# Router stage of a two-layer transformer step: the order of tile turns, adaLN parts, slot counts and gate spreads

## The reference, cut to what matters

```python
mod = silu(c) @ w_mod[l] + b_mod[l]          # 6 vectors of 1024: shift1, scale1, gate1, shift2, scale2, gate2
...
x = x + gate1 * (merged @ lp['w_out'])
h2 = rms_norm(x, lp['norm2_w']) * (1 + scale2) + shift2
y = grouped_moe(h2, router_w, router_b, w_g, w_u, w_d)
x = x + gate2 * y
...
def grouped_moe(h, router_w, router_b, w_g, w_u, w_d):
    s = sigmoid(h @ router_w)                # 16 experts in 4 groups
    sb = (s + router_b).reshape(T, 4, 4)
    # the group with the largest sum of its best two; in it the best two experts
    # w = s of these two, divided by their sum
    for e in range(16):
        y = y + gates[:, e:e+1] * ((silu(h @ w_g[e]) * (h @ w_u[e])) @ w_d[e])
```

## Time and profile before

| | us |
|---|---|
| median of 3 runs | 1649.46 (1648.64 to 1653.35) |
| span of the profiled execution | 1646.0 |
| PE busy | 1567.6 (95%) |
| DVE busy | 1047.2 (64%) |
| ACT busy | 923.8 (56%) |
| POOL busy | 530.5 (32%) |
| layer 0: end of dense matmuls, first expert matmul | 486.3, 524.7 |
| layer 1: the same | 1300.2, 1335.0 |

### The profile page before, as it was taken

The page is one execution under the profiler, slowest core; times in us unless marked ns, Lnnn a source line. Parts: engine busy times, 40 slices in busy tenths (PEclk is TensorE's granted clock), DMA queues, the critical chain, the costliest instruction groups (busy, mean ns, idle before and its releaser), DMA issues.

```text
span 1646.0 us, 21287 instructions
## 1 busy us (share of the span) xinstructions
PE 1567.6 (95%) x7693; PEld 1234.8 (75%) x7693; DVE 1047.2 (64%) x1385; ACT 923.8 (56%) x1284; POOL 530.5 (32%) x271
## 2 busy tenths in 40 slices
PE   7999999989999999999889999999999989999996
PEld 4677778877775887888676777787767778888885
DVE  2226546673355898998862357377433479899998
ACT  3343445434335788888644343444353458888893
POOL 2344554444532111111234445444445131111112
PEclk9999999999998999999999999999999999999998
DMA  9765343344359999999946543422443469999995
GB/s 363 265 199 167 115 128 91 102 130 143 115 174 334 344 385 362 370 377 364 368 170 210 187 154 112 133 90 89 144 147 111 157 224 379 378 368 378 381 368 205
DMA packets 153822, 381.77 MB, mean 232 GB/s; under 512 B 21060, under 2 KB 26886, under 8 KB 153724
## 3 DMA queue, kind: packets, MB, share of 16 engines
q1 hardware_dynamic: 122704, 325.32, 56.2%
q10 hardware_dynamic: 20140, 36.56, 6.3%
q0 software_dynamic: 10880, 18.59, 3.1%
HBM read 378.55 MB, written 27.93 MB: 247 GB/s over the span
## 4 chain that ended last, share of the span: by engine, by line
PE 70%; DVE 12%; DMA 10%; ACT 5%; issue 2%; ACTq 0%; SPq 0%; POOL 0%; DVEq 0%; POOLq 0%
PE ps L606 56%; PE ps L615 4%; DVE wxl L2466 4%; DMA raw<-w_e_down 4%; DMA raw<-w_e_up 3%; PE ps L639 2%; PE ps L952 2%; ACT wxh L1826 1%; DMA own<-w_mod 1%; PE ps L980 1%; PE ps L886 1%; DVE uv L2241 1%; ACT wh L1331 1%; PE ps L658 1%; PE ps L650 1%
## 5 line engine op out<-in xcount | busy, mean ns | idle before, releaser
L1949 POOL TENSOR_TENSOR wl<-raw,wh 128x1024 fp32r<-128x1024 f32 x168 | 409.8, 2443 | 531.7 <-ACT wh L1331 531.5
L2466 DVE TENSOR_TENSOR wxl<-raw,wxh 128x1024 fp32r<-128x1024 f32 x384 | 454.5, 1220 | 55.2 <-ACT wxh L1826 52.5
L1826 ACT ACTIVATE wxh<-raw 128x1024 fp32r<-128x1024 f32 x384 | 402.6, 1061 | 92.4 <-DMA raw<-w_e_down 35.4
L606 PE MATMUL ps<-wxh,xeT 128*128 128x512 f32 x1024 | 341.3, 399 | 4.0 <-issue 2.5
L1331 ACT ACTIVATE wh<-raw 128x1024 fp32r<-128x1024 f32 x168 | 176.7, 1056 | 227.6 <-PE ps L606 223.2
L606 PE MATMUL ps<-wh,hTh 128*128 128x512 f32 x720 | 293.2, 407 | 5.9 <-DVE hTl L2088 3.3
L606 PE MATMUL ps<-wh,hTl 128*128 128x512 f32 x720 | 281.9, 392 | 0.0
L606 PE MATMUL ps<-wl,hTh 128*128 128x512 f32 x720 | 281.5, 391 | 0.0
L606 PEld LDWEIGHTS ps<-wxh,xeT 128*128 128x128 f32 x1024 | 193.3, 189 | 46.8 <-issue 4.3
L606 PE MATMUL ps<-wxl,xeT 128*128 128x512 f32 x512 | 199.9, 390 | 0.0
L606 PEld LDWEIGHTS ps<-wh,hTh 128*128 128x128 f32 x720 | 135.7, 188 | 40.7 <-issue 7.9
(11 more groups left out here) (282 smaller groups left out, 2177.3 us busy)
## 6 DMA issues: line engine op xcount, KB each, us to landing
raw<-w_e_gate SPq DMA_DIRECT2D x128, 512.0 KB, 6.5
raw<-w_e_up SPq DMA_DIRECT2D x128, 512.0 KB, 5.8
raw<-w_e_down SPq DMA_DIRECT2D x128, 512.0 KB, 5.5
raw<-w_in SPq DMA_DIRECT2D x120, 512.0 KB, 3.7
own<-w_mod ACTq DMA_DIRECT2D x27, 1024.0 KB, 7.6
raw<-w_mod SPq DMA_DIRECT2D x36, 512.0 KB, 5.1
raw<-w_br_b SPq DMA_DIRECT2D x16, 512.0 KB, 3.8
raw<-w_out SPq DMA_DIRECT2D x16, 512.0 KB, 3.8
```

The costliest lines, as they stand in the source:

```text
L606: ins = pe.matmul(out, act_hl[i], w_hl[j], start=start and n == 0, stop=stop and n == 2)
L1826: act.activation(wxh[:, q % RING_MOE, :, :], raw[:, place, :, :], ACT.Copy).then_inc(sem("hi_done"), 1)
L1949: pool.tensor_tensor(wl[:, p % RING, :, :], raw[:, PAIR_CHUNK[p] % RAW, :, :], wh[:, p % RING, :, :].bitcast(F32), ALU.subtract).then_inc( ...
L2466: dve.tensor_tensor(wxl[:, q % RING_MOE, :, :], raw[:, expert_chunk(l, 0, q)[0], :, :], wxh[:, q % RING_MOE, :, :].bitcast(F32), ALU.subtr ...
```

## The change

The diff touches the router stage alone, in both layers, and no size. Tile t's turn now comes as soon as PE reaches it behind the dense matmuls, and the adaLN parts stand between the tiles. ACT takes all eight columns of tile 0 (`ACT_COLUMNS`), with a semaphore `tile_whole` for the last four, and works on tile 0 ahead of the third tile's squares; DVE keeps columns 4 to 7 of tiles 1 and 2. The sigmoid's table and the `iota` load now follow the last `tile_front`. In layer 0 parts of blocks 2 and 3 come behind the token logits; in layer 1 three of the four gate spreads come behind the token sums. `counts` comes right behind the third tile's `back` (layer 1, with four spins ahead) or behind part(3, 0) (layer 0).

```diff
-FILL_ROUTER = (4, 4, 4, 6, 16)
+FILL_ROUTER = (4, 16)
+ACT_COLUMNS = (8, 4, 4)
...
             # PE, ahead of everything else of the stage
-            if more:
-                part(0, 0)
-                part(0, 1)
-                part(1, 0)
-                part(1, 1)
-            else:
-                part(10, 0)
-                part(10, 1)
-                part(11, 0)
...
             # PE, the stage's order (more: layer 0)
+            turn_tile(0)
             if more:
-                turn_tile(0)
+                part(0, 0)
+                part(0, 1)
                 turn_tile(1)
+                part(1, 0)
                 turn_tile(2)
-                part(2, 0)
+                part(1, 1)
                 logits(0)
+                logits(1)
                 turn_small(l + 1)
+                logits(2)
                 block_columns(blocks, 0)
-                logits(1)
-                part(2, 1)
-                logits(2)
-                block_columns(blocks, 1)
-                part(3, 0)
                 token_logits()
                 back(0)
                 back(1)
+                block_columns(blocks, 1)
+                part(2, 0)
+                part(2, 1)
+                back(2)
+                part(3, 0)
+                counts()
                 part(3, 1)
-                back(2)
                 block_columns(blocks, 2)
-                counts()
                 part(10, 0)
                 block_columns(blocks, 3)
             else:
-                spin(FILL_ROUTER[0], 2)
-                turn_tile(0)
-                spin(FILL_ROUTER[1], 2)
+                part(10, 0)
                 turn_tile(1)
+                part(10, 1)
                 turn_tile(2)
-                part(11, 1)
                 logits(0)
                 logits(1)
+                part(11, 0)
+                logits(2)
+                back(0)
+                token_logits()
+                back(1)
+                part(11, 1)
+                back(2)
+                spin(FILL_ROUTER[0], 5)
+                counts()
                 block_gate(blocks, 10, 0, 0)
-                logits(2)
-                block_gate(blocks, 10, 1, 0)
-                token_logits()
-                back(0)
-                back(1)
-                block_gate(blocks, 11, 0, 1)
-                back(2)
-                block_gate(blocks, 11, 1, 1)
-                spin(FILL_ROUTER[2], 5)
-                counts()
-                spin(FILL_ROUTER[3], 5)
...
             # PE, behind token_sums of experts 0 and 1, layer 1
-                spin(FILL_ROUTER[4], 5)
+                block_gate(blocks, 10, 1, 0)
+                block_gate(blocks, 11, 0, 1)
+                block_gate(blocks, 11, 1, 1)
+                spin(FILL_ROUTER[1], 5)
...
             # ACT
-            for t in range(NT):
-                half_squares(1, t)
-                tile_root(NT + t)
-            act.dma_start(iota[:, :], io["t_iota"]).then_inc(sem("iota_in"), 16)
-            act.wait_ge(sem("col_ready"), at("col_ready", l, 2))
...
-            tile_front(0)
+            half_squares(1, 0)
+            tile_root(NT)
+            half_squares(1, 1)
+            tile_root(NT + 1)
+            act.wait_ge(sem("col_ready"), at("col_ready", l, 2))
+            tile_front(0, 0, 4)
+            half_squares(1, 2)
+            tile_root(NT + 2)
+            tile_front(0, 4, 8)
+            tile_front(1, 0, ACT_COLUMNS[1])
+            tile_front(2, 0, ACT_COLUMNS[2])
+            warm(l, ACT.Sigmoid)
+            act.dma_start(iota[:, :], io["t_iota"]).then_inc(sem("iota_in"), 16)
             block_row(blocks, 0 if more else 10)
-            tile_front(1)
             if more:
                 block_row(blocks, 1)
-            tile_front(2)
-            if not more:
-                block_row(blocks, 11)
-                gate_row(l, 10, 0, 0)
-            warm(l, ACT.Sigmoid)
-            if more:
-                block_row(blocks, 2)
-            else:
-                gate_row(l, 10, 0, 1)
             act.wait_ge(sem("tok_acc"), at("tok_acc", l, 1))
...
             for i in range(4):
                 row_copy(i)
+            block_row(blocks, 2 if more else 11)
+            row_copy(4)
+            row_copy(5)
             if more:
                 block_row(blocks, 3)
-            else:
-                gate_row(l, 11, 1, 0)
-            row_copy(4)
-            row_copy(5)
             act.wait_ge(sem("gate_ready"), at("gate_ready", l, 1))
...
-                gate_row(l, 11, 1, 1)
+                for n, bank in ((10, 0), (11, 1)):
+                    for g in range(2):
+                        gate_row(l, n, bank, g)
...
             # DVE
-                for k in range(4):
...
+                for k in range(ACT_COLUMNS[t], KD):
...
-            for t in range(NT):
+            for t in range(1, NT):
                 tile_back(t)
```

More of the change, by code:

```diff
@@ L1058, in turn_tile @@
                     pe.wait_ge(sem("tile_front"), at("tile_front", l, 1))
-                    pe.wait_ge(sem("tile_back"), at("tile_back", l, 1))
+                    pe.wait_ge(sem("tile_whole"), at("tile_whole", l, 1))
                 pe.wait_ge(sem("xn_done"), at("xn_done", l, NT + t + 1))
@@ L1071, in logits @@
                 for half in range(2):
-                    name = ("tile_front", "tile_back")[half]
-                    pe.wait_ge(sem(name), at(name, l, t + 1))
+                    if half == 0:
+                        pe.wait_ge(sem("tile_front"), at("tile_front", l, t + 1))
+                    elif t == 0:
+                        pe.wait_ge(sem("tile_whole"), at("tile_whole", l, 1))
+                    else:
+                        pe.wait_ge(sem("tile_back"), at("tile_back", l, t))
                     for j in range(4):
@@ L1091, in back @@
                     pe.wait_ge(sem("tile_front"), at("tile_front", l, t + 2))
-                    pe.wait_ge(sem("tile_back"), at("tile_back", l, t + 2))
+                    pe.wait_ge(sem("tile_back"), at("tile_back", l, t + 1))
                 for half in range(2):
@@ L1757, in scalar_program, with tile_front @@
                 half_squares(0, t)
-            for t in range(NT):
-                half_squares(1, t)
-                tile_root(NT + t)
-            act.dma_start(iota[:, :], io["t_iota"]).then_inc(sem("iota_in"), 16)
-            act.wait_ge(sem("col_ready"), at("col_ready", l, 2))
-            def tile_front(t):
+            def tile_front(t, first, end):
                 base, g = 2 if t == 1 else 6, min(t, 1)
-                act.wait_ge(sem("tile_turned"), at("tile_turned", l, 2 * t + 1))
-                for k in range(4):
-                    ins = act.activation(hT[:, t, k, :], ps[:, base, k * P:(k + 1) * P], ACT.Identity,
+                act.wait_ge(sem("tile_turned"), at("tile_turned", l, 2 * t + 1 + (end > 4)))
+                for k in range(first, end):
+                    ins = act.activation(hT[:, t, k, :], ps[:, base + k // 4, k % 4 * P:(k % 4 + 1) * P], ACT.Identity,
                                          scale=scl[:, 1, k, g:g + 1], bias=shf[:, 1, k, g:g + 1])
-                ins.then_inc(sem("tile_front"), 1)
+                ins.then_inc(sem("tile_front" if first < 4 else "tile_whole"), 1)
             def row_copy(i):
@@ L2399, in tile_back @@
                 dve.wait_ge(sem("tile_turned"), at("tile_turned", l, 2 * t + 2))
-                for k in range(4):
-                    ins = dve.tensor_scalar(hT[:, t, 4 + k, :], ps[:, base + 1, k * P:(k + 1) * P], scl[:, 1, 4 + k, g:g + 1],
-                                            shf[:, 1, 4 + k, g:g + 1], ALU.mult, ALU.add)
+                for k in range(ACT_COLUMNS[t], KD):
+                    ins = dve.tensor_scalar(hT[:, t, k, :], ps[:, base + k // 4, k % 4 * P:(k % 4 + 1) * P],
+                                            scl[:, 1, k, g:g + 1], shf[:, 1, k, g:g + 1], ALU.mult, ALU.add)
                 ins.then_inc(sem("tile_back"), 1)
-            for t in range(NT):
+            for t in range(1, NT):
                 tile_back(t)
```

2 lines of the change are left out of this document (1 added, 1 removed).

## The result

The changed kernel takes 1655.5 us (median of 20 runs, 1649.6 to 1664.3), the kernel before 1651.4 in 20 runs on the same chips (1643.1 to 1654.5): ratio 1.0033 (of the means), 95% interval 1.0020 to 1.0045, or 5.4 us slower; the medians are 4.0 us apart. The forecast was 1650.5 and "no change"; what came is close to the time of rival (a), 1654.8. The profiled executions are 1646.0 and 1654.6 us long, 8.6 apart, which is more than the medians: runs of one kernel scatter over some 10 us, so a profile is read for its places, and the runs give the price.

What follows compares the result with a forecast made beforehand. TensorE was taken as the limit (busy 95%), so shifts of the first expert matmul count. Layer 0 +4.5 and layer 1 -3.5 gave +1.0 on 1649.5: 1650.5 us, range 1644 to 1656.5, likeliest case 1646.5 to 1654.

Steps and rivals of the forecast that it cites:

- rival (a): Layer 0's adaLN stream becomes the bound, then half clock: +7.5 there, -2.2 in layer 1, 1654.8 us; chance 0.24.
- Tile turning: Both layers' router start: in layer 0 last logits 2.6 us earlier, sigmoid 1.6 us earlier.
- The stream: Layer 0's adaLN loads: block 3's second half issued 8.5 us later, PE waiting 2 to 3 us before part(3,1).
- The gate write: Layer 0's gate DMA, issued at 510.7: +3.1 if it takes 9.29 us again, off the path if 2.9.
- +4.5: Layer 0's loss as taken, in us, between the bounds +2.0 and +7.5.
- +2.0: Layer 0's lower bound in us: gathered rows turned at 524.3, no more slow-clock time than before.
- +7.5: Layer 0's upper bound in us: everything from part(3,1) to the last part at half rate, rows at 529.8.
- Layer 1: Layer 1's router: sigmoid 3.9, slots 7.2, gather's end 6.4 us earlier; spins end last, gathered rows' turn gains; -3.5 taken.
- up to 1.2 us more is lost: Layer 1, if the clock falls between the gate spreads: the gain shrinks to -2.2 us.
- the signs: Checks: load gap 494 to 503, idle before part(3,1), layer 0's first expert matmul 526 to 532, layer 1's turn 2 to 5 us nearer.
- (c): Rival: no effect on the path, layer 1's spins at half rate, layer 0 covered by 2.0; about 1651.5 us; 0.61 with forecast.
- (b): Faster rival: layer 0 about breaks even (-0.7), layer 1 gains -4.9 with the clock kept; 1643.9 us; chance 0.15.

Runs made afterwards that it cites:

- e13: Changed kernel with 17 never-executed fillers, fetching only a quarter of each `w_mod` load beside layer 0's router: ratio 0.9964 to the kernel before.
- e3: Changed kernel with layer 0's part(2,0) ahead of the token logits, part(2,1) behind them, part(3,0) ahead of the second back: ratio 1.0013 to before.
- e7: e3 with 17 never-executed fillers in layer 0's second pass over the experts: ratio 0.9987 to the kernel before.
- e10: Changed kernel with 17 never-executed fillers, layer 0's first four parts ahead of tile 0's turn, and e3's order: ratio 0.9999 to before.
- e16: Changed kernel with 17 never-executed fillers; layer 0: ScalarE's first row copy between tile evictions, parts 2 and 3 among logits and turns back, counts last: ratio 0.9968.
- e2: Changed order in layer 1 alone, layer 0 in the order of before: ratio 0.9996 to the kernel before.
- e11: e8 without layer 1's 16 live fillers behind the gate spreads: ratio 0.9962 to the kernel before.
- e6: Kernel before with 17 never-executed fillers in layer 0's second pass over the experts: ratio 0.9965 to the kernel before.
- e15: Kernel before with 4 never-executed fillers in layer 0's second pass: ratio 0.9980 to the kernel before.
- e17: Kernel before with 32 never-executed fillers in layer 0's second pass: ratio 0.9978 to the kernel before.
- e1: Changed order in layer 0 alone, layer 1 in the order of before: ratio 1.0042 to the kernel before.
- e5: Changed kernel with 17 never-executed fillers in layer 0's second pass: ratio 1.0017 to the kernel before.
- e8: e2 (layer 1 alone in the changed order) with 17 never-executed fillers in layer 0's second pass: ratio 0.9963 to the kernel before.

## Why the prediction was wrong

*Tile turning.* Right, and better than said: the dense matmuls ended 0.5 us sooner in the second profile, and behind that end the logits were copied 3.1 us earlier (494.48; forecast 2.6) and the sigmoid ran 3.0 earlier (497.30; forecast 1.6). The table load cost its 1.28 us and no drain.

*The stream.* The mechanism was as described: no load issued from 494.7 to 502.4, parts 2 done at 503.2 (forecast 504.0), 2.03 us of waiting before part(3,1) (2 to 3), slots at 506.32 (507.1), gates issued at 509.45 (510.7). That the issue times came out so well is partly luck: the sigmoid was 1.4 us better than forecast, and the two turns back behind it, at half clock, took 3.45 us instead of 1.94, which I had not foreseen. The gate write was off the path: 6.7 us from its issue, it landed at 516.2.

*Layer 0's sum.* **This is the step that failed**: "I take +4.5, between, since PE waits for DMA in part of it anyway", between the bounds +2.0 and +7.5. Measured: +8.3, beyond the upper bound. Of this, 4.3 us are idle time of PE and 4.0 are slower work. The +2.0 counts one wait, for the load of block 3 at the median landing of 5.7 us. The load behind it, the first half of block 10, was issued at 504.01, as forecast, but took 9.07 us to land, and PE stood another 2.92 us for it before part(10,0). At 5.7 us it would have been there at 509.7, ahead of PE: this wait is nowhere in my sum. And the half clock, priced at 2.5 (from +2.0 to +4.5), cost the 4.0: 1.5 in the two turns back and most of the rest in the late stretch, whose work at half clock took 13.4 us instead of 9.0. The discount was right in kind (of these 17.0 us at half clock PE was idle for 3.5), but what stood behind the wait ran at half rate as the upper bound had it.

e13 shows that the late stream is the cause of the waits. e3 and e7 show that the late place of parts 2 and 3 makes the stream late: with these early, both waits are gone. It is not all: with parts 2 and 3 early, too, e10 waits 1.05 and 2.61 us and e16 5.32. Why some loads took 9.07 or 12.13 us and others 5.7 is open.

*Layer 1.* Sigmoid and slots came about as forecast, the gather 4.3 us earlier instead of 6.4, since the gate write took 5.7 us where I had 2.9; PE was later still. But "up to 1.2 us more is lost" for a clock that falls between the spreads was too little: three spreads of 2.05 to 2.07 us instead of 1.0, and fillers of 4.38 instead of 3.82, make 3.7. The stage got 0.7 us shorter in the profiled runs (35.1 to 34.4), and e2 shows no gain in time, where I took -3.5. e11 shows that even the time spent in fillers isn't free to take.

*Sum.* At the experts' starts it is +8.3 - 0.7 = 7.6 where I had +1.0. The kernel lost 5.4 by the runs (3.3 to 7.4). That layer 0's expert phase gave the difference back is not shown: it was 6.0 us shorter in the profiled pair, but the phase of the kernel before was the longest of its kind there (300.4 us, against 296.8, 296.8 and 296.1 in e6, e15 and e17; the changed layer 0 has 296.1 in e1 and e5). With the fillers the sums agree better: e5's stages are 8.3 and 0.5 us longer than e6's, and the runs differ by 8.6.

Of the signs, the gap in the issues, the idle time before part(3,1) and layer 1's slots were right; the first expert matmul came just behind its window (532.46), and layer 1's turn came 0.6 us nearer to the dense end, not 2 to 5. Rival (a) had the place and should have had the larger chance: the half rate that it priced already stood in that place in the earlier trace rows. Its total is partly luck: layer 0 lost more than its 7.5 and layer 1 gained less than its 2.2, and the slow stretch began at the second wait and not at the first. (c) was right of layer 1 and wrong of layer 0, (b) wrong of both.

## What to carry to other kernels

Where a work item frees the buffer of a later load, its place in the order is the load's issue time: moving it behind a chain of waits moves every load behind it, and two of them were waited for here, not one. Behind an empty queue the late loads come all at once: price the second and third at the landing that a full queue gave in the old profile (9.29 us for the gates), not at the median. If a stretch of narrow matmuls already runs at half clock in the old profile, price a new idle there in full, and what it pushes into that stretch at half rate, not at a mean. Profile the kernel before more than once: the stage of one order scattered by 2.6 us, a third of what was to be explained. And let a wait that the profile shows as "issue" right behind a jump be compared with the packets of the instruction queue before any order of work is blamed for it.

## What the runs showed of the hardware

PE's code comes over the same DMA engines as the weights, in 16 KB packets that the trace lists. Behind this jump one packet came at once, with PE's first weights 2.6 to 2.7 us behind its start, and the next 3.3 to 5.3 us later, when the weights' transfers ran out (after: they took 0.9 of the 16 engines' time from 829.7 to 832.0). Where PE needed that second block, it stood for 2.63 us (before), 4.41 (after) and 4.73 (e17), of which the last 2.2 to 2.6 us lie behind the start of the packet. Seventeen filler matmuls that never run move the target; with them the kernel before takes 1643.1 us and layer 1's changed order on top of it 1643.2 (e8; 1643.9 without its live fillers, e11), against 1648.2 and 1649.8 for the kernel before beside them: these three, equal within their intervals, beat both kernels. How much of that the stall explains is open (e15 and e17).
